# Input rows transposed unscaled, the norm's root applied later as a broadcast row of scales

## What is computed

```python
h = rmsnorm(x, norm_mix_g)                       # x * rsqrt(mean(x*x) + eps) * g
u_rnn, g_rnn, u_pool, q_mem = split(h @ w_in)    # 512, 512, 256, 256 channels
y_rnn = rg_lru(causal_conv(u_rnn)) * gelu(g_rnn)
y_pool = multiscale_pool(u_pool)
k, v = split(rmsnorm(mem, mem_norm_g) @ w_mem_kv)
y_mem = attention(q_mem, k, v)                   # 4 heads, 256 memory rows
x = x + concat(y_rnn, y_pool, y_mem) @ w_out
x = x + moe_ffn(rmsnorm(x))                      # top 4 of 32 experts
out = rmsnorm(x)
```

## Time and profile before

| | |
|---|---|
| median of three runs | 1742.33 us (1741.3 to 1746.7) |
| profiled execution | 1749.63 us, of which its span 1748.0 us |
| PE, DVE, ACT, POOL busy | 96%, 75%, 63%, 25% of the span |
| mean granted clock of PE | 0.981 |
| mixer, up to the first expert product | about 345 us, then 35 us of preparation |
| chain that ended last, PE's share | 69% |

### The profile page before, as it was taken

The page is one execution under the profiler, slowest core; times in us unless marked ns, Lnnn a source line. Parts: engine busy times, 40 slices in busy tenths (PEclk is TensorE's granted clock), DMA queues, the critical chain, the costliest instruction groups (busy, mean ns, idle before and its releaser), DMA issues.

```text
span 1748.0 us, 29388 instructions
## 1 busy us (share of the span) xinstructions
PE 1677.2 (96%) x8625; PEld 1253.4 (72%) x8626; DVE 1304.2 (75%) x1167; ACT 1102.7 (63%) x1066; POOL 445.7 (25%) x348
## 2 busy tenths in 40 slices
PE   7999999859999999999999999999999999999996
PEld 6877788736786767888867887678667767665674
DVE  5578656566787778899878997769668669665687
ACT  5464555355676666787766886667656657654674
POOL 5000001332322323222225132125213126123240
PEclk9999999869999999999999999999999999999998
DMA  9121132467898989999989998799868788787685
GB/s 276 56 96 61 49 109 73 150 237 287 327 343 325 343 292 346 373 389 376 389 324 358 380 389 312 283 347 369 312 263 288 298 322 328 299 321 251 230 325 217
DMA packets 114175, 485.71 MB, mean 278 GB/s; under 512 B 16430, under 2 KB 29040, under 8 KB 81360
## 3 DMA queue, kind: packets, MB, share of 16 engines
q1 hardware_dynamic: 96128, 445.58, 65.8%
q0 software_dynamic: 18000, 39.49, 9.3%
HBM read 451.79 MB, written 33.23 MB: 277 GB/s over the span
## 4 chain that ended last, share of the span: by engine, by line
PE 69%; DVE 4%; issue 2%; DMA 2%; ACT 1%; POOLq 0%; ACTq 0%; DVEq 0%; POOL 0%; SPq 0%
PE ps L1812 19%; PE ps L1814 18%; PE ps L1813 18%; PE ps L1827 6%; PE ps L1865 3%; DVE w_lo L1656 3%; PE ps L1785 2%; DMA raw_weights<-in_w_down 1%; PE ps L1835 1%; ACT w_hi L1510 1%; PE ps L1890 1%; DVE raw_weights L1757 0%; PE ps L1794 0%; DMA stand_in<-token_lists 0%; DVE xT L1662 0%
## 5 line engine op out<-in xcount | busy, mean ns | idle before, releaser
L1656 DVE TENSOR_TENSOR w_lo<-raw_weights,w_hi 128x2048 fp32r<-128x2048 f32 x256 | 577.2, 2285 | 135.8 <-ACT w_hi L1510 135.6
L1510 ACT ACTIVATE w_hi<-raw_weights 128x2048 fp32r<-128x2048 f32 x256 | 486.0, 1911 | 224.4 <-DMA raw_weights<-in_w_gu 102.2
L1812 PE MATMUL ps<-w_hi,xT 128*128 128x512 f32 x1024 | 415.5, 406 | 12.2 <-issue 6.3
L1813 PE MATMUL ps<-w_lo,xT 128*128 128x512 f32 x1024 | 403.3, 394 | 0.0
L1814 PE MATMUL ps<-w_hi,xT 128*128 128x512 f32 x1024 | 402.5, 393 | 0.0
L1656 DVE TENSOR_TENSOR w_lo<-raw_more,w_hi 128x2048 fp32r<-128x2048 f32 x128 | 290.1, 2285 | 29.9 <-ACT w_hi L1510 29.8
L1812 PEld LDWEIGHTS ps<-w_hi,xT 128*128 128x128 f32 x1024 | 194.0, 189 | 93.4 <-issue 47.1
L1510 ACT ACTIVATE w_hi<-raw_more 128x2048 fp32r<-128x2048 f32 x128 | 244.0, 1907 | 0.0
L1436 POOL DMA_INDIRECT x_rows<-h_rows,next_list x33 | 79.7, 2415 | 614.7 <-issue 614.7
L1814 PEld LDWEIGHTS ps<-w_hi,xT 128*128 128x128 f32 x1024 | 194.2, 190 | 42.8
L1813 PEld LDWEIGHTS ps<-w_lo,xT 128*128 128x128 f32 x1024 | 194.3, 190 | 36.7
(11 more groups left out here) (314 smaller groups left out, 2150.4 us busy)
## 6 DMA issues: line engine op xcount, KB each, us to landing
raw_weights<-in_w_gu SPq DMA_DIRECT2D x192, 1024.0 KB, 8.7
raw_more<-in_w_gu SPq DMA_DIRECT2D x64, 1024.0 KB, 6.4
raw_weights<-in_w_down SPq DMA_DIRECT2D x64, 1024.0 KB, 9.6
raw_more<-in_w_down SPq DMA_DIRECT2D x64, 1024.0 KB, 11.9
rows<-in_x SPq DMA_DIRECT2D x12, 512.0 KB, 4.9
w_in_sb<-in_w_in SPq DMA_DIRECT2D x12, 512.0 KB, 4.1
acc_rows<-region_c SPq DMA_DIRECT2D x8, 512.0 KB, 2.6
h_rows<-region_c SPq DMA_DIRECT2D x8, 512.0 KB, 3.9
```

Source lines behind the costliest of these rows:

```text
L1510: S.activation(w_hi[:, j % RING, :], raw(j % RING), ACT.Copy).then_inc(hi_done, 1)
L1656: V.tensor_tensor(w_lo[:, j % RING, :], raw(j % RING), w_hi[:, j % RING, :].bitcast(F32), ALU.subtract).then_inc(lo_done, 1)
L1812: T.matmul(out, hi, hi_w, start=first, stop=False)
L1813: T.matmul(out, hi, lo_w, start=False, stop=False)
```

## The change

- PE transposes the raw row tiles with an identity (`T.transpose`) as soon as they have landed; `row_scale` and `scales` are gone. All ten row tiles have buffers of their own (three more in `mixedT`), and SP issues their loads without waiting. The loads of the small vectors (`vrows`) move from POOL's queue to ACT's.
- ACT evacuates both high halves of a tile, DVE both low ones; DVE's copy L711 is gone. ACT squares tile 0 first and tiles 1 to 9 only after `w_in_hi(1)`. `project_half(0, 0)` is cut in four pieces that stand between the transposes of tiles 4 to 7.
- `row_roots` (DVE) makes all roots at once and two sets of diagonal matrices, `row_scales` (PE) multiplies them with a matrix of ones, which gives a row of roots copied to all partitions, and `row_scales` (ACT) copies it to SBUF (`rs_row`, `mem_scale`).
- DVE multiplies by that row where it evacuates u, g and the pool channels (`u_evac`, `g_evac`, `pooled_evac`, by `scaled`), and the keys (`keys_evac`). ACT's `u_evac` and `pooled_evac` are gone; its GeLU (`gate_of`) now works in place on what DVE's `g_evac` left. ACT scales the values (`v_sb`); the queries' root enters the exponent's scale (`q_scale`).
- `w_mem_kv` is loaded after the seventh square; the keys wait for the roots' row; `w_out` piece 3 is loaded after the pool evacuations, since its buffer holds `rs_row`.

Left out of the diff below: renamed semaphores, `row_in`, `vector_rows` moved as it is, `u_evac`, `pooled_evac` and `keys_evac` (made like `g_evac`), the removed bodies on ACT, and the exponent's scale.

```diff
-        row_slots = [rows[:, i, :] for i in range(3)] + [region_d[:, i * D:(i + 1) * D] for i in range(4)]
+        row_slots = [rows[:, i, :] for i in range(3)] + [region_d[:, i * D:(i + 1) * D] for i in range(4)]\
+            + [mixedT[:, i, :] for i in range(3)]
...
-            for item in range(len(row_slots)):
+            for item in range(TT // 2):
                 load_rows(item)
-            for n in range(3):
-                load_w_in(n)
-                sp.wait_ge(xT_ready, n + 1)
-                load_rows(len(row_slots) + n)
-            sp.wait_ge(xT_ready, len(row_slots))
+            load_w_in(0)
+            for item in range(TT // 2, TT):
+                load_rows(item)
+            load_w_in(1)
+            for item in range(TT, NORMED):
+                load_rows(item)
+            load_w_in(2)
+            sp.wait_ge(xT_ready, 7)
+            sp.wait_ge(ss_done, 7)
             sp.dma_start(w_kv_sb, dram["w_mem_kv"][0].rearrange("(k p) n -> p k n", p=P)).then_inc(kv_in, 16)
...
+            sp.wait_ge(pu_done, 2 * PT_)
+            load_w_out(3)
...
             def x_hi(s):
+                for b in range(2):
+                    nc.scalar.activation(hi_part[:, 4 * b:4 * b + 4, s * P:(s + 1) * P],
+                                         bank(4 + 2 * (s % 2) + b)[:, 0, :].rearrange("p (k t) -> p k t", k=4),
+                                         ACT.Copy).then_inc(x_hi_done, 1)
+            def row_scales():
+                act.wait_ge(rs_row_ready, 1)
+                nc.scalar.activation(rs_row, bank(6, 2).rearrange("p b n -> p (b n)"), ACT.Copy).then_inc(rs_row_done, 1)
+                for m in range(MT):
+                    nc.scalar.activation(mem_scale[m], bank(5)[:, 0, m * P:(m + 1) * P], ACT.Copy).then_inc(rs_row_done, 1)
...
+            act.wait_ge(pool_step, 3)
+            for r, n, src in vector_rows:
+                act.dma_start(vrows[r:r + n, :], src).then_inc(vrows_in, 16)
             act.preload_act_table(ACT.Sqrt)
             square(0)
-            square(1)
-            act.wait_ge(consts, 1)
-            root(0)
-            for s in range(NORMED):
-                if s + 2 < NORMED:
-                    square(s + 2)
-                if s + 1 < NORMED:
-                    root(s + 1)
-                row_scale(s)
-                if 1 <= s <= TT:
-                    x_hi(s - 1)
-                if s == 5 or s == 7:
-                    w_in_hi((s - 5) // 2)
+            for s in range(TT):
+                x_hi(s)
+                if s == 4:
+                    w_in_hi(0)
+            w_in_hi(1)
+            for s in range(1, NORMED):
+                square(s)
+            act.wait_ge(ms_done, 1)
+            nc.scalar.activation(sd[:, 0:NORMED], ms[:, 0:NORMED], ACT.Sqrt).then_inc(sd_done, 1)
             act.wait_ge(lam_abs, 1)
             nc.scalar.activation(lam[:, 1, :], lam[:, 0, :], ACT.Exp, scale=-1.0).then_inc(lam_exp, 1)
-            act.wait_ge(pads_zero, 2)
-            act.wait_ge(zero_out, 32)
-            act.wait_ge(table_set, 16)
-            act.wait_ge(vec_done, 1)
-            act.wait_ge(lam_done, 2)
-            def u_evac(c):
-                if c:
-                    act.wait_ge(conv_done, c)
+            row_scales()
...
+            def gate_of(c):
                 for h in range(2):
+                    act.wait_ge(g_scaled, 2 * c + h + 1)
+                    half = g_t[:, h * HALF:(h + 1) * HALF]
+                    nc.scalar.activation(half, half, ACT.Gelu_apprx_tanh).then_inc(gelu_done, 1)
...
                 root_of(c - 1)
-                u_evac(c)
                 w_in_hi(2 * c + 2)
-                g_evac(c)
+                gate_of(c)
                 w_in_hi(2 * c + 3)
                 gate_values(c)
-            pooled_evac(0, 0)
             root_of(RT - 1)
-            pooled_evac(0, 1)
             w_in_hi(N_Q)
             act.preload_act_table(ACT.Exp)
-            pooled_evac(1, 0)
-            pooled_evac(1, 1)
...
+            def row_roots():
+                dve.wait_ge(ss_done, NORMED)
+                V.tensor_scalar(ms[:, 0:NORMED], ss[:, 0:NORMED], 1.0 / D, EPS, ALU.mult, ALU.add).then_inc(ms_done, 1)
+                dve.wait_ge(sd_done, 1)
+                link(V.reciprocal(rs[:, 0:NORMED], sd[:, 0:NORMED]))
+                V.tensor_tensor(rs_diag, ident[:, :].unsqueeze(1).broadcast_to([P, TT, P]),
+                                rs[:, 0:TT].unsqueeze(2).broadcast_to([P, TT, P]), ALU.mult).then_inc(diag_done, 1)
+                V.tensor_tensor(mem_diag, ident[:, :].unsqueeze(1).broadcast_to([P, MT, P]),
+                                rs[:, TT:NORMED].unsqueeze(2).broadcast_to([P, MT, P]), ALU.mult).then_inc(diag_done, 1)
+                link(V.tensor_scalar(q_scale, rs[:, 0:TT], HD ** -0.5, None, ALU.mult))
...
-                        if b:
-                            link(V.tensor_copy(hi_part[at], src))
-                        else:
-                            dve.wait_ge(x_hi_done, s + 1)
+                        dve.wait_ge(x_hi_done, 2 * s + b + 1)
                         V.tensor_tensor(lo_part[at], src, hi_part[at].bitcast(F32), ALU.subtract).then_inc(xT_done, 1)
...
+            def scaled(out, n, h, signal):
+                dve.wait_ge(proj_ready, 2 * n + h + 1)
+                cols = slice(h * HALF, (h + 1) * HALF)
+                V.tensor_tensor(out[:, cols], bank(2 * (n % 2) + h)[:, 0, :], rs_row[:, cols], ALU.mult).then_inc(signal, 1)
...
+            def g_evac(c):
+                if c:
+                    dve.wait_ge(rnn_done, c)
+                for h in range(2):
+                    scaled(g_t, 2 * c + 1, h, g_scaled)
...
-            mean_square(0)
-            mean_square(1)
-            row_scale(0)
-            for s in range(NORMED):
-                if s + 1 < NORMED:
-                    row_scale(s + 1)
-                if s + 2 < NORMED:
-                    mean_square(s + 2)
-                if s == 3:
+            for s in range(TT):
+                xT_evac(s)
+                if s == 2:
                     vector_columns()
                     dve.wait_ge(vec_done, 1)
-                if s:
-                    xT_evac(s - 1)
-                if s == 6 or s == 8:
-                    w_in_lo((s - 6) // 2)
+                if s == 4:
+                    w_in_lo(0)
+            w_in_lo(1)
             scale(2)
-            xT_evac(NORMED - 1)
-            scale(3)
...
+            row_roots()
+            scale(3)
...
+            u_evac(0)
             conv(0)
+            g_evac(0)
             dve.wait_ge(b_gu_hi_done, 1)
             V.tensor_tensor(b_gu_lo[:, :, :], b_gu_raw[:, :, :], b_gu_hi[:, :, :].bitcast(F32), ALU.subtract)\
                 .then_inc(b_gu_lo_done, 1)
             w_in_lo(2)
             scale(4)
+            keys_evac()
...
+                    u_evac(c + 1)
                     conv(c + 1)
                 w_in_lo(2 * c + 4)
                 if c + 1 < RT:
                     scale(2 * c + 6)
+                    g_evac(c + 1)
...
+            pooled_evac(0)
             pool_windows(0)
             w_in_lo(N_Q + 1)
+            pooled_evac(1)
...
-                pe.wait_ge(xn_done, s + 1)
+                pe.wait_ge(row_in(s)[0], row_in(s)[1])
                 if s >= 2:
                     pe.wait_ge(xT_done, 2 * (s - 1))
                 for k in range(KT):
-                    last = T.matmul(bank(4 + 2 * (s % 2) + k // 4)[:, 0, (k % 4) * P:(k % 4 + 1) * P],
-                                    row_tile(s)[:, k * P:(k + 1) * P], scales[:, s % 2, :], start=True, stop=True)
+                    last = T.transpose(bank(4 + 2 * (s % 2) + k // 4)[:, 0, (k % 4) * P:(k % 4 + 1) * P],
+                                       row_tile(s)[:, k * P:(k + 1) * P], ident[:, :])
...
+            def row_scales():
+                pe.wait_ge(diag_done, 2)
+                pe.wait_ge(xT_done, 2 * NORMED)
+                pe.wait_ge(consts, 8)
+                for h in range(2):
+                    T.matmul(bank(6 + h)[:, 0, :], ones[:, :], m_t[:, h * HALF:(h + 1) * HALF], start=True, stop=True)
+                T.matmul(bank(5)[:, 0, 0:MT * P], ones[:, :], uc[:, 0:MT * P], start=True, stop=True).then_inc(rs_row_ready, 1)
...
-                if s >= TT - 1 and s < NORMED - 1:
-                    project_half(0, s - TT + 1)
+                if s >= TT // 2:
+                    k = 2 * (s - TT // 2)
+                    project_half(0, 0, range(k, k + 2))
+            project_half(0, 1)
+            transpose_rows(TT)
+            project_half(1, 0)
+            transpose_rows(TT + 1)
+            project_half(1, 1)
+            row_scales()
...
-                pe.wait_ge(xT_done, 2 * NORMED)
+                pe.wait_ge(rs_row_done, 1 + MT)
...
-                        pe.wait_ge(kv_done, 2)
+                        pe.wait_ge(kv_done, 2 * MT)
```

168 lines of the change are left out of this document (80 added, 88 removed).

## The result

| | before | after |
|---|---|---|
| median of four runs | 1742.12 us (1741.3 to 1746.7) | 1759.82 us (1759.2 to 1760.7) |
| profiled execution | 1749.63 us | 1760.10 us |
| mean granted clock of PE | 0.981 | 0.975 |
| first expert instruction on PE | 371.94 us | 377.04 us |
| last expert instruction on PE | 1733.65 us | 1744.04 us |

The ratio is 1.0091, with a 95% interval of 1.0063 to 1.0120: slower, where 1744.3 with a range of 1737 to 1753 was forecast. The profiled pair differs by 10.5 us: 5.1 us are there when the experts begin, 5.3 come up behind that, in a phase whose code the change does not touch. Four profiled executions with the mixer of the kernel before begin the experts at 371.40 to 372.41 us, the changed kernel's three at 377.04, 377.17 and 375.02.

A forecast was written before the change was run, and what follows sets the result against it. PE, busy 96% of the span, was taken as the bound. Profiled 1749.6 us, minus 3.7 in the opening, plus 5.7 in the loop, gave 1751.6, and with that execution 7.3 above the median, 1744.3 us; range 1737 to 1753.

The forecast's parts named there:

- The opening: Mixer's start up to `project(2)`: transposing raw tiles starts PE earlier; `project(2)` at 69.3 instead of 73.0 us, gaining 3.7 us.
- T: Start of `project_half(0, 1)` on PE in the opening, forecast at 29.8 us, or 26.4 us at full pace throughout.
- hardly: PE's wait at `gates(1)` in the loop: claimed to be hardly any, against 2.8 us at `gates(2)` and at `gates(3)`.
- the GeLU's table: Rival, ACT in the loop: table loaded behind its wait, 1.28 us more per chunk, 1746.9 us; chance 0.18.
- The loop: Mixer's chunks: `g_evac` late on DVE delays ACT's GeLU; sigmoids 28.06 instead of 25.25 us apart, PE loses 5.7 us.
- that case: Clock falls at `gates(2)`: PE is 1.7 us later at `gates(3)`, whose wait shrinks by as much; nothing added.
- Its other case: Clock falls at `gates(3)` instead, after the wait of 2.8 us there: 1.7 us are added.
- nothing else is changed in length: Everything behind the mixer's loop keeps its length, so no term was added there.
- time won or lost on PE in the mixer should reach the end one to one: First expert product waits for the whole mixer, so the mixer's change on PE was carried whole into the kernel's time.
- The base: Starting point of the sum: profiled execution of 1749.6 us, taken as 7.3 us above the median.
- transposes do not raise the clock: Rival, opening: transposes don't count as PE work, so tiles 5 to 7 run slow; 6.7 us more, 1751.0 us; chance 0.17.
- the fast case: Rival: opening at full pace gains 7.1 us, DVE's new evacuations cost the loop nothing; 1735.2 us; chance 0.15.

The follow-up runs named there:

- a_wearly: Changed kernel with only ACT's five waits moved ahead of `w_in_hi(3)` and the value rows' copies; one execution, 1753.98 us.
- a_again: The changed kernel, unaltered, measured again beside the kernel before: 1756.49 us against 1747.40 us.
- a_gfirst: Changed kernel with only DVE's order changed back, `g_evac` of the next chunk directly behind its `conv`; one execution, 1754.67 us.
- a_free144: Changed kernel plus 144 do-nothing PE instructions, spread over two idle times, restoring the expert code's place: 1752.61 us, ratio 1.0029.
- b_pad112: Kernel before plus 112 executed do-nothing PE instructions ahead of the expert phase's first transpose: 1755.21 us, ratio 1.0037.
- b_jump112: Kernel before plus 112 PE instructions ahead of the expert phase's first transpose, nearly all filler that is jumped over: 1755.55 us, ratio 1.0039.
- a_order_free144: Changed kernel with `g_evac` directly behind `conv`, ACT's five waits earlier, and 144 do-nothing PE instructions in two idle times: 1744.57 us, ratio 0.9982.
- a_order: Changed kernel with DVE's `g_evac` directly behind `conv` and ACT's five waits ahead of the value rows' copies, no filler: 1753.02 us, ratio 1.0033.
- b_jump256: Kernel before plus 256 PE instructions (16 KB) ahead of the expert phase's first transpose, nearly all filler jumped over: 1753.18 us, ratio 1.0008.

## Why the prediction was wrong

**The opening: right in its steps, missed at its end.** Pieces at 18.7 for 18.9, T at 30.25 for 29.8, every distance from T to the keys within 0.11 us. The DMAs took ACT 1.48 to 4.62 us, 0.25 to 0.57 each, where 0.45 was taken. `keys_evac` made PE wait 0.68 for 0.4. So `project(2)` came 2.8 us earlier than before instead of 3.7. The missing term is the next one: I set the first sigmoid at 69.9, as if its table stood loaded. The change puts five waits between the values' copies and the sigmoid, the load stays behind them, and it stands behind PE's release too: 1.28 us on the path. `gates(1)` then waited 1.35 us, where I had "hardly". I had asked this question of the GeLU's table, and there the answer was as I took it (in chunk 1 the load at 83.18 stands ahead of a wait of 12.3 us); I had not asked it of the sigmoid. a_wearly moved the load, got back 0.93 to 1.9 us, and had no wait at `gates(1)`.

**The loop: right.** From one chunk's first sigmoid to the next 28.09 us for 28.06, PE's loss 5.67 us for 5.7, the wait at `gates(2)` 2.57 for 2.8. The clock fell at `gates(2)` (eight products in 5.40 us) and the wait at `gates(3)` shrank to 0.88 us, as the text said for that case. Its other case is a_again: there the wait at `gates(2)` brought no slow stretch and that at `gates(3)` did, and from `gates(3)` to the last h2 tile PE needed 193.11 us instead of 191.42, the 1.7 us that the text adds for it. The cause is shown by a_gfirst: two instructions' difference in DVE's order.

**Behind the loop: a small term.** The mixer's end moved from 4.39 to 4.94 us late, the first expert instruction 5.10. The step "nothing else is changed in length" was off by 0.7 us. Up to the last h2 tile it is 0.55, which I have not taken apart. Behind it two idles nearly cancel: the one ahead of the unit table's columns is 1.2 us longer than in before (5.60 for 4.38), the one ahead of the first expert instruction 1.05 shorter (14.16 for 15.21).

So the mixer lost 5.1 us where my sum said 2.0 (the other two executions of the changed kernel: 5.2 and 3.1; a_free144, timed: 5.1 with 0.5 to 9.6).

**The step that failed** is "time won or lost on PE in the mixer should reach the end one to one". It has no term for the code itself. Taking 144 instructions out of PE's program moved the code of the expert loop against the 16 KB pieces in which it is fetched, and some 6.5 us went into branches that wait for code: b_pad112 +6.5 us (2.8 to 10.1) and b_jump112 about as much, with nothing of the change in them. Mixer and place together make 11.6 us, and the two larger measurements of the changed kernel say 12.4 and 10.8 by their ratios.

**The base.** I set my sum against a median of three runs, 1742.3, and called the profiled 1749.6 an execution 7.3 us above it. Over 116 runs the median is 1747.5, and 43% of them lie at or under 1746.7, where all of the first four did. That is chance in some 3 cases of 100, so luck is likely but not shown; another chip or hour is not ruled out. Of the 15.5 us between 1744.3 and 1759.8, about 5 are this, 3 the mixer, 6.5 the place; the remaining microsecond is within any of these intervals. Without the place and the base the sum would still have been 3 us short, within the range.

**The rivals.** That transposes do not raise the clock did not hold. The windows of the kernel after:

```profile
13.60:17.10 3.50, 1.10 (x8) 0.86 (x8) 2.51 (x5) 2.60 (x5) 1.90 (x1) 1.00 1.00 390
17.10:23.90 6.80, 5.20 (x16) 4.41 (x17) 1.40 (x2) 0.82 (x3) 3.70 (x6) 0.50 1.00 312
```

Up to 13.6 us PE had run nothing but transposes, and from there the clock was 1.00, 2.4 GHz: the tile at 14.23 took 1.10 us. (The Trainium skill, "TensorE: Matmul & The Clock Gate", section "Part 4: PE-mode transpose", says the full clock does not engage for them; this trace disagrees.) It was low again after the idle of 3.38 us, so the first pieces ran slow, as forecast, for another reason than the rival's. The GeLU's table and the fast case did not happen.

## What to carry to other kernels

An edit that changes the number of instructions on an engine with a large branching loop moves the loop's code. Before a few microseconds are explained by the edit, put the same number of idle instructions into the old kernel, or back into the new one, where the engine waits anyway; the packets of the instruction queue and the idle times marked "issue" at branches show at once whether the place has changed. Where one engine takes over an evacuation from another, its place among the instructions ahead of it can cost more (2.27 us a chunk here) than the work itself (0.57). A wait that is set directly ahead of a function's first use also pins its table load there.

## What the runs showed that I had not expected

- A branch of PE whose code has to be fetched takes 3.3 to 5.9 us, against 0.07 to 0.4, and the idle it causes can also halve the clock: for 4.3 us of work behind the idle of 6.59 us.
- At a bad place such fetches come late in the loop and in every one of the nine executions seen (20 packets behind 1240 us). At a good place the early ones vary between executions and kernels: 8 to 13 packets from 360 to 700 us, two to four long branches. The timed runs spread more there: a_order_free144 from 1735.7 us at a mean clock of 0.982 to 1755.4 at 0.975, b_pad112 only from 1752.5 to 1757.7. That the early fetches make this spread is likely, but only one run of each kernel has a trace.
- Idle times under the 3.00 us of the earlier trace rows can lower the clock, but need not: ten waits of 2.57 to 2.61 us ahead of `gates(2)` or `gates(3)`, in six executions, made the eight products behind them slow (5.40 us) five times and left them at 3.70 us five times. The same kernel, a_again, has both:

```profile
121.63 3.70 PE L1122 MATMUL ps<-region_c,blockdiag 128*128 128x512 f32 x8 [2.59 <-DVE region_c L809]
...
149.71 5.40 PE L1122 MATMUL ps<-region_c,blockdiag 128*128 128x512 f32 x8 [2.60 <-DVE region_c L809]
```

- After the 2.29 us ahead of the last h2 tile that tile took 1.97 us in before, the changed kernel, a_gfirst and a_order, but 1.09 in a_wearly, b_jump112 and b_jump256. It is worth nothing: PE's next wait is 3.10 us there for 2.2 in the others.
- A wait that is already fulfilled occupies PE for 0.106 us; 144 of them are 15.3 us.

What stays open: why the first use of a body is fetched in some executions and not in others, which piece displaces which, and how many pieces an engine can hold. No run here changed the size of the loop. A kernel that beats the one before by more than its interval was not found: with the order mended and the place restored the change is worth -3 us (-8 to +1.6).
